# Second block's mixer as one list of steps, with input tiles and a diagonal-matrix convolution tile between the attention's rounds

## The reference, cut to what matters

```
u = rmsnorm(h) @ w_in                     # 1024 -> 2560: value, gate, q, k, v, 512 each
glu = value * sigmoid(gate)
y = depthwise causal conv of width 31 over glu, + conv_b
conv_out = silu(layernorm(y))             # over the 512 channels of a position
z = q k^T / 8, strict causal mask, 8 heads of 64
attn = exp(log_sigmoid(z) + sum of log_sigmoid(-z) over the keys between)
attn_out = rmsnorm per head (attn @ v)
h = h + rmsnorm([conv_out, attn_out] @ w_out)
```

## Time and profile before

| what | value |
|---|---|
| median of 3 runs | 1988.01 us (1985.15 to 1995.7) |
| profiled execution, its own time | 1984.31 us |
| its span in the trace | 1982.5 us |
| TensorE busy | 1831.3 us, 92% |
| VectorE, ScalarE, GpSimd busy | 1006.7, 764.2, 240.8 us |
| mean granted clock of TensorE | 0.958 |

### The profile page before, as it was taken

How to read it: one execution, slowest core, us unless ns; L and a number is a source line. 1 busy time by engine, 2 the same in 40 slices (tenths; PEclk the granted TensorE clock), 3 DMA queues, 4 the chain that set the end, 5 groups by cost and what they waited for, 6 DMA issues and landing times.

```text
span 1982.5 us, 21540 instructions
## 1 busy us (share of the span) xinstructions
PE 1831.3 (92%) x8356; PEld 1490.9 (75%) x8356; DVE 1006.7 (51%) x1702; ACT 764.2 (39%) x1506; POOL 240.8 (12%) x238
## 2 busy tenths in 40 slices
PE   7899999999999997889999999986796989999995
PEld 6777788888887776667888888765575768888884
DVE  5555443344335556555343344588787354244344
ACT  6332242323325555444232323543464443332232
POOL 0011010100101011001010100254234000000000
PEclk9999999999999999899999999998787989999998
DMA  6222323333332111012333333222100323333331
GB/s 224 74 64 64 96 85 102 101 96 96 96 96 81 51 54 43 28 37 85 100 92 103 99 96 96 85 54 63 43 1 0 96 69 102 96 96 96 96 96 43
DMA packets 195749, 158.37 MB, mean 80 GB/s; under 512 B 5248, under 2 KB 161152, under 8 KB 195648
## 3 DMA queue, kind: packets, MB, share of 16 engines
q1 hardware_dynamic: 194240, 154.16, 25.9%
q0 software_dynamic: 400, 1.25, 0.2%
...
HBM read 154.88 MB, written 2.10 MB: 79 GB/s over the span
## 4 chain that ended last, share of the span: by engine, by line
PE 78%; DVE 15%; ACT 3%; issue 2%; DMA 0%; POOL 0%; ACTq 0%; DVEq 0%
PE ps L686 26%; PE ps L688 24%; PE ps L687 24%; DVE sb L2110 4%; DVE sb L1716 2%; PE ps L737 1%; ACT sb L1218 1%; DVE sb L2235 1%; DVE sb L2172 1%; DVE sb L2182 1%; PE ps L1101 0%; DVE sb L1714 0%; DVE sb L1876 0%; PE ps L1004 0%; DVE sb L1742 0%
## 5 line engine op out<-in xcount | busy, mean ns | idle before, releaser
L686 PE MATMUL ps<-sb,sb 128*128 128x512 f32 (+3 forms) x2516 | 989.6, 396 | 68.3 <-DVE sb L1716 22.1
L688 PE MATMUL ps<-sb,sb 128*128 128x512 f32 (+3 forms) x2516 | 964.2, 385 | 0.0
L687 PE MATMUL ps<-sb,sb 128*128 128x512 f32 (+3 forms) x2516 | 964.0, 385 | 0.0
L686 PEld LDWEIGHTS ps<-sb,sb 128*128 128x128 f32 (+1 forms) x2516 | 479.3, 192 | 182.7 <-DVE sb L1716 31.3
L688 PEld LDWEIGHTS ps<-sb,sb 128*128 128x128 f32 (+1 forms) x2516 | 479.5, 192 | 93.4
L687 PEld LDWEIGHTS ps<-sb,sb 128*128 128x128 f32 (+1 forms) x2516 | 480.8, 192 | 85.4
L1716 DVE TENSOR_TENSOR sb<-sb,sb 128x512 fp32r<-128x512 f32 x532 | 363.3, 724 | 357.0 <-ACT sb L1218 356.0
L1218 ACT ACTIVATE sb<-sb 128x512 fp32r<-128x512 f32 x532 | 304.9, 622 | 443.4 <-PE ps L688 443.2
L1915 DVE TENSOR_TENSOR sb<-sb,sb 128x512 fp32r<-128x512 f32 x64 | 68.1, 1064 | 177.0 <-ACT sb L1360 177.0
L569 POOL TENSOR_TENSOR sb<-sb 128x512 f32<-128x512 f32 x64 | 66.9, 1045 | 606.6 <-ACT sb L1370 606.6
L1370 ACT ACTIVATE sb<-ps 128x512 f32<-128x512 f32 x64 | 38.3, 598 | 208.3 <-PE ps L688 208.3
...
## 6 DMA issues: line engine op xcount, KB each, us to landing
...
```

What stands on the lines that cost most here:

```text
L686: mm(ps, lh, rh, start=start, stop=False, **k)
L687: mm(ps, lh, rl, start=False, stop=False, **k)
L688: return mm(ps, ll, rh, start=False, stop=stop, **k)
```

## The change

The mixer's steps up to the output product are now one list, `PLAN_C`, that all four compute programs walk through; each does its own part of a step. With line numbers of the new file left out, this is what changes:

- The input tiles come in the order g0 v0 g3 v3 g1 v1 g2 q0 k0, then `v2` into banks 4 to 7. The other seven (q1, v2, k1, q2, k2, q3, k3) go one at a time through bank 7 between the attention's steps ("tile" in `EARLY` and `LATE`). Here "v2" is both the value tile of group 2 and, as `("v2", j)`, a slab of the attention's values.
- 93 taps of groups 0 to 2 are VectorE's; ScalarE's and GpSimd's taps are gone. Group 3 is made by TensorE: the weights of each tap stand on the diagonal of a 128 x 128 matrix (high half DH by ScalarE, low half DL by GpSimd), multiplied with the shifted GLU tile in 31 `mm3`, in groups of 10, 10 and 11 ("dg", "cv"), with sixteen buffers of matrices. They lie in Ah and Al.
- ScalarE does the rounding of SP and AT at 1408 columns; VectorE takes the low half whole; GpSimd has no part in it. One buffer LN_ in place of two.
- Everything that passes through bank 7 waits for the eviction of the step before it there (`free_7`).
- The pair's product is rounded by ScalarE into M2h, now in Ah, and waits there for the last input tile, k3.
- The layernorm stands behind the last head's round: variance sums as 16 products of two columns, inverse root on 4 columns, spread by transposes. Pair 3 is finished ahead of the output product, whose slabs are taken in the order [4,5], [0,1], [2,3], [6,7].

```diff
-    for j in range(4):
-        SL["in", 2 * j] = slab([(w2, 512 + j * 128, 128)], 0, 8)
-        SL["in", 2 * j + 1] = slab([(w2, j * 128, 128)], 0, 8)
-    for j in range(8):
-        SL["in", 8 + j] = slab([(w2, 1024 + j * 128, 128)], 0, 8)
+    IN_FIRST = ["g0", "v0", "g3", "v3", "g1", "v1", "g2", "q0", "k0"]
+    IN_LATER = ["q1", "v2", "k1", "q2", "k2", "q3", "k3"]
...
-        CH["out", n] = chunk([(W["w_out_2"][0], 512 * n, 512)], by(2))
+        CH["out", n] = chunk([(W["w_out_2"][0], 512 * n, 512)], [[4, 5], [0, 1], [2, 3], [6, 7]])
...
+    CV_GROUPS = [range(0, 10), range(10, 20), range(20, 31)]
+    TAPS = [(j, k) for j in range(3) for k in range(31)]
+    for n, x in enumerate(IN_FIRST):
+        PLAN_C += [("tile", x), ("lo", x)]
+        PLAN_C += [("taps", 5 if n >= 2 else 0)]
+    for j in range(4):
+        PLAN_C += [("v2", j), ("taps", 4)]
+    PLAN_C += [("v2_out",)]
+    EARLY = {0: [("tile", "q1"), ("lo", "q1")], 4: [("tile", "q3"), ("lo", "q3")]}
+    LATE = {0: [("tile", "v2")], 1: [("tile", "k1"), ("lo", "k1")], 2: [("tile", "q2"), ("lo", "q2")],
+            3: [("tile", "k2"), ("lo", "k2")], 4: [("tile", "k3"), ("lo", "k3"), ("dg", 0)], 5: [("cv", 0), ("dg", 1)],
+            6: [("cv", 1), ("dg", 2)], 7: [("cv", 2)]}
+    for u in range(10):
+        if u < 8:
+            PLAN_C += [("lg", u)]
+        if u == 8:
+            PLAN_C += [("ln_sub",)]
+        if u >= 4 and u % 2 == 0:
+            PLAN_C += [("ps", u // 2 - 2), ("pr", u // 2 - 2)]
+        if u == 9:
+            PLAN_C += [("ln_mul",)]
+        PLAN_C += EARLY.get(u, [])
+        if u >= 2:
+            PLAN_C += [("va", u - 2)]
+        PLAN_C += [("taps", 3)]
+        if u < 8:
+            PLAN_C += [("sp", u)]
+        if 1 <= u <= 8:
+            PLAN_C += [("bt", u - 1)]
+        if u == 8:
+            PLAN_C += [("ln_var",), ("ln_rs",)]
+        if u >= 4 and u % 2 == 0:
+            PLAN_C += [("pt", u // 2 - 2), ("pl", u // 2 - 2)]
+        PLAN_C += [("taps", 3 if u < 7 else 100)]
+        if 1 <= u <= 8:
+            PLAN_C += [("at", u - 1)]
+        PLAN_C += LATE.get(u, [])
+    PLAN_C += [("ln_lo",), ("ps", 3), ("pr", 3), ("pt", 3), ("pl", 3)]
...
-    SLOW = [(0, q) for q in range(31)] + [(2, q) for q in range(16)]
-    TAPS = [(1, q) for q in range(31)] + [(3, q) for q in range(31)] + [(2, q) for q in range(16, 31)]
...
+            elif step[0] == "dg":
+                for k in CV_GROUPS[step[1]]:
+                    if k >= 16:
+                        q.wait_ge(S("cv_used"), 1 + ((k - 16) >= 10))
+                    else:
+                        q.wait_ge(S("w_used"), SL["in", "k3"] + 1)
+                    q.wait_ge(S("cw"), 2)
+                    e.tensor_scalar(DL[:, k % 16, :], IDENT, CWL[:, k:k + 1], None, ALU.mult).then_inc(S("dl"), 1)
...
+        def conv_group(g):
+            taps = CV_GROUPS[g]
+            q.wait_ge(S("cv_g"), 1)
+            for k in taps:
+                q.wait_ge(S("dh"), k + 1)
+                q.wait_ge(S("dl"), k + 1)
+                x = slice(k, k + T)
+                m = mm3(banks[7][:, :], DH[:, k % 16, :], DL[:, k % 16, :], GLH[:, x], GLL[:, x], k == taps[0],
+                        k == taps[-1])
+            m.then_inc(S("cv_used"), 1)
...
+            elif kind == "pl":
+                p = a[0]
+                q.wait_ge(S("pair_n"), p + 1)
+                q.wait_ge(S("w_used"), SL["in", "k3"] + 1)
+                act(M2h[:, 4 + p, :], TN, ACT.Copy).then_inc(S("pair_hi"), 1)
```

More of the change, by code:

```diff
@@ L708, in tile_n @@
         def tile_n(c, xh, xl, ready, b0, free, turn=no_step, step=no_step, behind=no_step):
-            k0, rows, n = 0, sum(c.kts), c.n
-            for j, kt in enumerate(c.kts):
+            n, order = c.n, [k for ks in c.ks for k in ks]
+            for j, ks in enumerate(c.ks):
                 i, wh, wl = next_slab()
@@ L728, in tile_n @@
                     behind(j, t)
-                k0 += kt
         def turned(job):
@@ L1546, in scalar_program @@
-        c = CH["v2"]
-        for j in range(4):
-            weights(c.first + j + 3)
-            slow_taps(2)
-        for t in range(4):
-            q.wait_ge(*tile_of(c, t))
-            act(VZh[:, t, :], banks[t][:, :], ACT.Copy, scale=rms("pre_mix", t, 1)).then_inc(S("vz_hi"), 1)
-        slow_taps(40)
-        def pair_square(p):
-            q.wait_ge(S("keep"), 2 * p + 2)
-            q.wait_ge(S("pair_lo"), p)
-            act(OQ, OSs[p % 2][:, :], ACT.Square).then_inc(S("pair_sq"), 1)
@@ L1571, in scalar_program @@
[L1571 to L1588 removed]
+        act(CWH[:, :], COL[:, cols["convw"] + 3:cols["convw"] + 124:4], ACT.Copy).then_inc(S("cw"), 1)
@@ L2119, in vector_program @@
-        for n in range(16):
-            weights(SL["in", n] + 3)
-            if n >= 4:
-                taps(4)
-            if n > 8:
-                qk_lo(n - 1)
-            ps = banks[n % 4][:, :]
-            q.wait_ge(S("w_used"), SL["in", n] + 1)
-            q.wait_ge(S("spread"), 2)
-            if n < 8 and n % 2 == 0:
-                q.wait_ge(S("glu"), n // 2 - 1)
-                tt(T4[:, n // 2 % 2, :], ps, RB[:, :], ALU.mult).then_inc(S("in_ev"), 1)
-            elif n < 8:
-                j = n // 2
+                else:
+                    stt(CV[:, j, :], GL[:, j, k:k + T], col("convw", 4 * k + j), CV[:, j, :], ALU.mult, ALU.add).then_inc(
+                        S("tap"), 1)
@@ L2158, in vector_program @@
[L2158 to L2169 removed]
+                i = QK.index(x)
```

598 lines of the change are left out of this document (312 added, 286 removed).

## The result

| kernel | median | lowest to highest | ratio to before, 95% interval |
|---|---|---|---|
| before, 11 runs | 1987.51 us | 1984.41 to 1995.70 | |
| after, 11 runs | 2003.01 us | 1997.35 to 2009.07 | 1.0076 [1.0058, 1.0094] |

The change makes the kernel 15 us slower. My forecast of 1992 with its range from 1966 to 2016 holds that time, but the case I thought likeliest, a time within 9.9 us of before, did not come about: 11 us of the 15 were not in my sum. The profiled execution took 2003.01 us.

What follows compares the result with a forecast made beforehand. TensorE, busy for 92% of the span, was taken as the bound. The output product ending its wait at 1537.4 against 1531.85 gave +5.5 - 1.6 = +3.9 us, so 1988.2, and with 3.7 for the median 1992, range 1966 to 2016.

Steps and rivals of the forecast that it cites:

- my sum: Ledger of engine times from the third eviction through the output product: +3.9 us against before; given 42%.
- rival (c): VectorE's taps before v2 do not get cheaper, since something other than GpSimd slowed them: 2025 us, 6%.
- The ring of 15.6 us: Attention rounds: VectorE and ScalarE steps in one fixed order sum to 15.6 us, just over TensorE's 13.7 to 14.4.
- s(2) to s(3): From head 2's to head 3's three additions that begin the softplus: an ordinary round, predicted 15.6 us.
- s(3) to s(4): From head 3's to head 4's softplus additions: round with the first pair's root and tile q3, predicted 22.6 us.
- s(4) to s(5): From head 4's to head 5's softplus additions: chain through bank 7, k3 and Ah, predicted 33.8 us.
- s(5) to s(6): From head 5's to head 6's softplus additions: nothing but diagonals delays ScalarE, predicted 14.9 us.
- The sixth round's 8.5 us: Second convolution group, 30 products after the pair leaves bank 7: 6.7 us, 8.5 with some at the lower clock.
- the 9.1 us charged ahead of the channel sums: Behind the last head's softplus additions: the third convolution group on TensorE delays the channel sums by 9.1 us.
- (a): Attention clock stays at 0.77, so a round with a tile lasts 17.8 us instead of 15.6: 2008 us, 26%.
- s(1) to s(2): From head 1's to head 2's softplus additions: an ordinary round, predicted 15.6 us.
- (b): Added waits overlap, some 5 us in each of rounds 3, 4, 6 and 10 in the tail: 1967 us, 26%.

Runs made afterwards that it cites:

- x1: The kernel after, with logits of heads 2 to 7 reading q and k of the pair before, so none waits for a fresh tile: 1990.75 us.
- x3: The kernel after with only one of the 31 convolution taps on TensorE left, the others dropped with their diagonals: 1992.77 us.
- x2: The kernel after with late tiles a step earlier (k1 ahead of v2, k2 early and q3 late in round 3), same computation: 1991.21 us.

## Why the prediction was right, and where not

**The bound and the input stage: right.** VectorE was the engine that ended `v2`: the values' low halves end at 1344.75, 64.4 us after the third eviction (65.5 predicted), and `q1` starts behind a wait of 3.75 us for them. A tap without GpSimd takes 0.78, as the earlier trace rows had it, so rival (c), taps that stay at 1.5, is out. VectorE's timeline, five taps with none of GpSimd's products beside them, five with one, and the values' low halves:

```profile
1300.88 3.89 DVE L2174 SCALAR_TENSOR_TENSOR sb<-sb,sb,sb 128x512 f32<-128x512 f32 x5
...
1306.50 4.81 DVE L2174 SCALAR_TENSOR_TENSOR sb<-sb,sb,sb 128x512 f32<-128x512 f32 x5
...
1342.03 2.72 DVE L2218 SCALAR_TENSOR_TENSOR sb<-ps,sb,sb 128x512 fp32r<-128x512 f32 x4
```

The 0.9 us that GpSimd's product adds is the 0.8 of the sum.

**The rounds: the term that failed.** The ring of 15.6 us put the logits beside the tile's eviction and copy, and the wait of logits for a tile just made at nothing. For odd heads that holds nearly: s(2) to s(3) took 16.9. For heads 2 and 4 the logits stand behind it, since they read the tile itself. Up to the end of ScalarE's copy of `k1`, at 1378.4, the round took the 11 us of the ring. There the ring had 4.4 more, for Abs, Exp and Ln. Measured were 10.0: the tile's low half, 0.7, the logits up to the last bank, which after 7 us of idling take 5.8 us from 1379.20 (3.7 at the full clock), and the last Abs, Exp and Ln, 3.5. That is 21.0 instead of 15.6. In s(3) to s(4) the same happened, with a second payment: tile `q3`, which my sum had beside other steps, follows those logits and the pair's sums, and took 8.2 us from 1424.69, half of it at the lower clock, against 5.4 at the full one. Together the two rounds are 14.8 over. x1 takes the wait out and leaves 2.9 too much, in the round with the pair. The wait could be read in the code and the plan before any run, in `qk_lo` and the place of `k1` and `k2` in `LATE`; I had listed the tiles' waits for bank 7 and not the waits for the tiles.

**s(4) to s(5): the mechanism right, 2.1 too long.** ScalarE stood 10.22 us at L1668 and VectorE 8.86 behind it, as the chain through bank 7 and Ah had it. Ten diagonals took 3.02, not 3.9, and GpSimd's low halves, for which I had added 2.5, hardly disturbed VectorE: three taps lasted 2.43 beside them instead of 2.32.

**s(5) to s(6): 1.9 short.** I had written that "nothing but diagonals delays ScalarE", but the pair's root stands in VectorE's order ahead of the round's three taps, and waits 4.84 us for a small ScalarE step queued behind Ln:

```profile
1483.12 0.17 DVE L1791 TENSOR_TENSOR sb<-sb 128x8 f32<-128x8 f32 x1 [4.84 <-ACT sb L1308]
...
1483.61 2.32 DVE L2174 SCALAR_TENSOR_TENSOR sb<-sb,sb,sb 128x512 f32<-128x512 f32 x3
```

**The convolution's price: half right.** The sixth round's 8.5 us were there (x3 took 7.7 out), and the diagonals' 3.0. Of the 9.1 us charged ahead of the channel sums, and 0.7 for the addition, at least 3.3 were on the path: by so much the pair's sums come earlier with the third group gone (x3). For the whole 45.1 us up to the output product I had 47.4.

**The output product: 3.2 better** than I had it, 48.2 us from its start to the MLP's first transpose against 53.0 before.

**The rivals.** (a), a falling clock, was in part what happened, not as I had put it. A table by stages for s(2) to s(3), where no tile is waited for, and for s(3) to s(4):

```profile
1388.00:1405.00 17.00, 17.00 (x94) 14.31 (x93) 11.75 (x15) 10.62 (x15) 0.00 (x0) 0.96 0.11 32
1405.00:1437.00 32.00, 25.39 (x104) 20.21 (x103) 14.66 (x23) 14.44 (x22) 0.00 (x0) 0.73 0.11 34
```

The round with a tile and no wait holds 0.96; the one with the long wait has 0.73. By the Trainium skill (TensorE: Matmul & The Clock Gate, Part 1) activity lifts the throttled clock, and these two rows agree. A wait is not needed for a lower clock, though: from s(0) to s(1) TensorE is busy for 11.01 of 11.01 us at 0.85. The sign I had given for (a), a clock under 0.88 with rounds over 17 us, came up in the rounds with long waits, as s(1) to s(2), 21.0 us at 0.69, and not in s(2) to s(3). From the third eviction to the output product the mean clock is 0.84 in after and in before. So the clock added to the price of the two waits and was no cause of its own: with the waits away (x1), the two rounds without a pair had the length of my ring. (b), overlapping waits, showed in the tail and in s(4) to s(5), 2 us each, far from its 25. Of the loss of 15 us, my sum had 4; the wait for the fresh k tile, 12 us by x1 and x2, makes up the rest. That the range held the time is owed to its width of 50 us, and the forecast would have been further off if the two long rounds, 14.8 over, had not been met by errors the other way: 2.1 in s(4) to s(5) and 5.5 behind s(7).
